# Down products of three feed-forward blocks: one 512-column matmul for both parts of the product, and its two halves added in two steps

## What is computed

```python
# first block
h = causal_dwconv(hn @ w_ffn_up[l], conv_w[l], conv_b[l])
x = x + (jax.nn.silu(h_gate) * h_val) @ w_ffn_down[l]
...
# second block, twice (g = g1 and g3)
x = x + 0.5 * g[:, None, :] * ((jax.nn.silu(gate) * up) @ w_out)
```

## Time and profile before

| | |
|---|---|
| median of 3 runs | 937.09 us (935.77 to 937.66) |
| profiled execution: time | 928.86 us |
| its span (first to last instruction) | 927.1 us |
| PE busy | 878.5 us (95%), 7320 matmul records |
| DVE busy | 710.3 us (77%) |
| ACT busy | 468.2 us (51%) |
| mean granted TensorE clock | 0.984 |
| w_lo (L1218) | x282, mean 1231 ns |
| w_hi (L841) | x282, mean 1052 ns |
| HBM read | 189.89 MB, 206 GB/s over the span |

### The profile page before, as it was taken

How to read it: one execution, slowest core, us unless ns; L and a number is a source line. 1 busy time by engine, 2 the same in 40 slices (tenths; PEclk the granted TensorE clock), 3 DMA queues, 4 the chain that set the end, 5 groups by cost and what they waited for, 6 DMA issues and landing times.

```text
span 927.1 us, 19318 instructions
## 1 busy us (share of the span) xinstructions
PE 878.5 (95%) x7320; PEld 842.5 (91%) x7320; DVE 710.3 (77%) x1104; ACT 468.2 (51%) x723; POOL 91.0 (10%) x139
## 2 busy tenths in 40 slices
PE   8999998999999988999999979899998979999996
PEld 6888997999999988999999869888998979999995
DVE  4898765999898778788888777678977878866543
ACT  5746654655664457334433455555643754434441
POOL 1022002000001320001012230000000200000010
PEclk9999999999999999899999999999999989999998
DMA  7453345566668974688889947745576347666651
GB/s 254 140 172 98 121 153 204 163 199 185 198 193 294 340 264 139 199 290 297 283 280 324 313 144 245 231 139 183 185 266 222 127 155 249 203 193 204 212 164 46
DMA packets 53334, 191.72 MB, mean 207 GB/s; under 512 B 5920, under 2 KB 6432, under 8 KB 53152
## 3 DMA queue, kind: packets, MB, share of 16 engines
q1 hardware_dynamic: 41760, 149.96, 49.1%
q0 software_dynamic: 10656, 39.33, 12.5%
q10 hardware_dynamic: 864, 1.67, 0.5%
HBM read 189.89 MB, written 1.05 MB: 206 GB/s over the span
## 4 chain that ended last, share of the span: by engine, by line
PE 76%; DVE 14%; ACT 5%; issue 3%; DMA 1%; SPq 0%; DVEq 0%; ACTq 0%
PE ps L388 22%; PE ps L390 22%; PE ps L389 22%; DVE w_lo L1218 5%; ACT w_hi L841 3%; DVE ada_raw L1520 2%; PE ps L460 1%; PE ps L462 1%; PE ps L461 1%; PE ps L496 1%; PE ps L553 1%; DVE rstd_w L1223 1%; DMA X<-x_in 1%; PE ps L527 1%; ACT xn L897 1%
## 5 line engine op out<-in xcount | busy, mean ns | idle before, releaser
L1218 DVE TENSOR_TENSOR w_lo<-raw,w_hi 128x1024 fp32r<-128x1024 f32 x282 | 342.0, 1231 | 114.2 <-ACT w_hi L841 113.8
L388 PE MATMUL ps<-xh,w_hi 128*128 128x256 f32 x1344 | 379.2, 282 | 19.2 <-DVE xl L1277 9.8
L389 PE MATMUL ps<-xl,w_hi 128*128 128x256 f32 x1344 | 374.8, 279 | 0.0
L390 PE MATMUL ps<-xh,w_lo 128*128 128x256 f32 x1344 | 374.7, 279 | 0.0
L841 ACT ACTIVATE w_hi<-raw 128x1024 fp32r<-128x1024 f32 x282 | 287.4, 1052 | 42.7 <-PE ps L390 38.8
L388 PEld LDWEIGHTS ps<-xh,w_hi 128*128 128x128 f32 x1344 | 255.8, 190 | 24.3 <-issue 21.1
L389 PEld LDWEIGHTS ps<-xl,w_hi 128*128 128x128 f32 x1344 | 255.5, 190 | 0.4 <-issue 0.2
L390 PEld LDWEIGHTS ps<-xh,w_lo 128*128 128x128 f32 x1344 | 255.2, 190 | 0.0
L388 PE MATMUL ps<-act_hi,w_hi 128*128 128x256 f32 x528 | 147.2, 279 | 5.0 <-DVE w_lo L1218 4.5
L390 PE MATMUL ps<-act_hi,w_lo 128*128 128x256 f32 x528 | 146.5, 277 | 0.0
L389 PE MATMUL ps<-act_lo,w_hi 128*128 128x256 f32 x528 | 146.5, 277 | 0.0
(11 more groups left out here) (259 smaller groups left out, 1140.8 us busy)
## 6 DMA issues: line engine op xcount, KB each, us to landing
raw<-w SPq DMA_DIRECT2D x282, 512.0 KB, 4.3
ada_raw<-ada_w POOLq DMA_DIRECT2D x72, 512.0 KB, 5.1
X<-x_in SPq DMA_DIRECT2D x4, 256.0 KB, 5.7
bm<-bias_in POOLq DMA_DIRECT2D x1, 1024.0 KB, 6.3
out<-X SPq DMA_DIRECT2D x4, 256.0 KB, 2.2
tab<-tab_in ACTq DMA_DIRECT2D x1, 640.0 KB, 4.2
gmask<-gmask_in ACTq DMA_DIRECT2D x1, 512.0 KB, 5.4
cact<-c_in POOLq DMA_DIRECT2D x1, 512.0 KB, 4.9
```

The lines of the kernel that those rows point to most:

```text
L388: pe.matmul(o, lh, rh, start=start, stop=False, skip_group_check=True)
L389: pe.matmul(o, lh, rl, start=False, stop=False, skip_group_check=True)
L390: return pe.matmul(o, ll, rh, start=False, stop=stop, skip_group_check=True)
L1218: v.tensor_tensor(w_lo[:, slot(h), :], raw[:, slot(h), :], w_hi[:, slot(h), :].bitcast(F32), ALU.subtract).then_inc(lo_ready, 1)
```

## The change

The two tensors act_hi and act_lo become one, `act`, in which the high and the low part of a hidden tile stand side by side (512 columns). PE multiplies w_hi by both with one matmul of 512 columns into the whole bank: columns 0 to 255 take w_hi x act_hi, columns 256 to 511 take w_hi x act_lo. The matmul w_lo x act_hi adds to columns 0 to 255 as before. So a weight tile has two matmuls and two weight loads in place of three, with 768 streamed columns as before, and the two halves of the bank have to be added together. That is done in `ffn_resid`: the left half is added to X, DVE waits for that addition to be complete, and then adds the right half to the same tile of X. Only the second addition signals `resid_done`, for which ACT's square waits.

```diff
-        ffn = phase([("act_hi", [P, FT, S], F32R), ("act_lo", [P, FT, S], F32R), ("cv", [P, 2, 2, SW], F32),
+        ffn = phase([("act", [P, FT, 2, S], F32R), ("cv", [P, 2, 2, SW], F32),
...
-        act_hi, act_lo, cv, sg, av, _, xr_h, xr_l, _, gain_sq, _, ada_raw, cact = ffn.values()
+        act, cv, sg, av, _, xr_h, xr_l, _, gain_sq, _, ada_raw, cact = ffn.values()
+        act_hi, act_lo = act[:, :, 0, :], act[:, :, 1, :]
...
-                    m = three(ffn_out(o), w_hi[:, slot(h), wc], w_lo[:, slot(h), wc], act_hi[:, ft, :], act_lo[:, ft, :], ft == 0, ft == FT - 1)
+                    pe.matmul(ps[:, 4 + o % 4, :], w_hi[:, slot(h), wc], act[:, ft, :, :].rearrange("p a n -> p (a n)"), start=ft == 0, stop=False, skip_group_check=True)
+                    m = pe.matmul(ffn_out(o), w_lo[:, slot(h), wc], act_hi[:, ft, :], start=False, stop=ft == FT - 1, skip_group_check=True)
...
-                if gate is None:
-                    v.tensor_tensor(X[:, o, :], ffn_out(o), X[:, o, :], ALU.add).then_inc(resid_done, 1)
-                else:
-                    v.scalar_tensor_tensor(out=X[:, o, :], in0=ffn_out(o), scalar=mod[:, gate, 16 + o:17 + o], in1=X[:, o, :],
-                                           op0=ALU.mult, op1=ALU.add).then_inc(resid_done, 1)
+                for part in range(2):
+                    src = ps[:, 4 + o % 4, part * S:part * S + S]
+                    if gate is None:
+                        ins = v.tensor_tensor(X[:, o, :], src, X[:, o, :], ALU.add)
+                    else:
+                        ins = v.scalar_tensor_tensor(out=X[:, o, :], in0=src, scalar=mod[:, gate, 16 + o:17 + o], in1=X[:, o, :],
+                                                     op0=ALU.mult, op1=ALU.add)
+                    if part == 0:
+                        own.mark(ins)
+                        own.wait()
+                ins.then_inc(resid_done, 1)
```

## The result

| | before | after |
|---|---|---|
| median of 20 runs each | 934.01 us (922.27 to 941.84) | 941.5 us (934.21 to 947.06) |
| ratio, with its 95% interval | | 1.012 (1.0096 to 1.0144) |
| profiled execution: time, span | 928.86, 927.1 us | 947.06, 945.3 us |
| mean granted TensorE clock | 0.984 | 0.981 |

The change makes the kernel slower by 1.2%, which on 934.01 us is 9.0 to 13.5 us; the two medians are 7.5 us apart, a ratio of 1.008, just outside that interval, so the size is less sure than the interval says. 943.9 us was forecast. The runs of one kernel spread by 1 to 2%, far more than the first three runs let me think. The profiled execution of the changed kernel is the slowest of its 20, and that of the kernel before is a quick one, so I read stages and not the 18.2 us between the two spans.

A forecast was written before the change was run, and what follows sets the result against it. A ring of DVE and ACT was taken to bound the first two down stages, PE the third. 3.2 + 3.8 + 0.5 - 0.7 = +6.8 us on a 937.09 us median gave 943.9 us, range 940.0 to 948.0.

The forecast's parts named there:

- the ring of ACT and DVE: First two down stages: addition, square, w_hi, w_lo set the pace, slower than PE; turns of 9.11 and 9.37 us.
- The second addition, first stage: First down stage: tiles 0 to 6 each pay 0.46 us ahead of PE's restart, tile 7 nothing; +3.2 us.
- Second stage: Second down stage: the second addition costs 0.52 us a tile, only 0.14 at tile 5 beside a transfer; +3.8 us.
- End of the third stage: Third down stage: only tile 7's second addition, behind PE's last matmul, costs; +0.5 us, tiles 0 to 6 hidden.
- The matmuls: Third down stage: a 512-column matmul takes 222 ns, a gain of 4 ns in each of 176 tiles; -0.7 us.
- The clock falls further: Rival: PE's longer waits bring more slow stretches, or wide matmuls cost 232 ns and later stages settle at 118; 947 us, chance 0.12.
- The layout: Writing act_hi and act_lo: same widths, same two instructions, only the distance between tiles changes; zero cost.
- In the first two stages the matmuls cost 0: First and second down stage: a faster PE only waits longer at the same w_lo; 0.
- PE decides after all: Rival: in the down stages additions lie beside PE except at stage ends, and matmuls gain; 931.6 us, chance 0.03.
- Half hidden: Rival: slots and transfers swallow most second-stage additions, or the first stage loses only its last tiles; 941 us, chance 0.12.
- It does not do what it says: Rival: the 512-column matmul runs as two of 256 at 226 ns, third stage gains nothing; 944.6 us, no separate chance.

The follow-up runs named there:

- e3: The kernel before with ACT's square of a finished tile moved behind the next w_hi, nothing else; 914.93 us, ratio 0.9842.
- e1: The changed kernel with three 256-column matmuls again, so only the second addition is left; 941.16 us against 929.43 for the kernel before, ratio 1.0127.
- e8: The changed kernel with a third DVE instruction that waits for the second addition and releases ACT in its place; 947.08 us in one run.
- run 20: Not a run label but a count: the kernel before, unchanged, was run 20 times; median 934.01 us.
- e2: The changed kernel with the 512-column matmul but only the first of the two additions; 932.45 us, ratio 1.0024 to the kernel before.
- e4: The changed kernel with ACT's square moved behind the w_hi of the next half; 925.4 us, ratio 0.9949 to the kernel before.
- e5: e4 with the wide matmul reading its 512 columns as two separate pieces; 927.29 us against 931.26 for the kernel before, ratio 0.9948.
- e9: e1 with ACT's square moved as in e3; 921.16 us against 930.93 for the kernel before, ratio 0.9886.
- e6: e4 with the w_lo matmul of each weight tile put in front of the wide one; 919.1 us in one run.
- e10: e3 again, the kernel before with the square moved, run beside e9; 916.98 us, ratio 0.9857 to the kernel before.
- e7: The kernel before profiled once more, without an edit; 931.31 us in one run.

## Why the prediction was right, and which term was mis-sized

**The bound.** That the ring of ACT and DVE sets the pace of the first two down stages, though PE holds 76% of the chain, is shown: take the square out of it and they are 3.1 and 5.3 us shorter (e3); lengthen it by 0.46 us and every turn grows by that (after, e1, e8).

**The second addition, first stage:** +3.2 forecast. PE's stage grew by 66.1 - 63.2 = 2.9 and the idle time behind it by 0.27, +3.2 together. Pair distance 0.46 and turn 9.56 (9.6 forecast) are as read from rows 3 and 8.

**Second stage:** +3.8 forecast. From the first scaling of X to the end of the last addition it was 539.3 - 484.0 = 55.3 us and is 555.3 - 495.6 = 59.7, +4.4. All eight additions are paid in full, 8 x 0.52 = 4.2: the 0.38 us of slack that I took off at tile 5 was not used. The turn is 9.88 (9.9 forecast). At the second transfer the wait stays, 1.15 us ahead of ACT's w_hi at 546.18 and 0.40 us on DVE behind it, as in rows 6 and 7:

```profile
546.18 1.06 ACT L843 ACTIVATE w_hi<-raw 128x1024 fp32r<-128x1024 f32 x1 [1.15 <-DMA raw<-w]
```

The transfer started later with the ring, as argued; it swallowed nothing of the additions ahead of it.

**End of the third stage:** +0.5 forecast, 1.00 - 0.48 = 0.52 in the row at 934.10. Additions of tiles 0 to 6 were to cost nothing there: e1's third stage is 59.5 us, as before.

**The matmuls: the step that failed in size, and in sign.** "I take 222 ns, a gain of 4 ns a tile: -0.7 us" was wrong. A wide and a narrow matmul take 353 ns, 13 more than three narrow ones at 113, and the third stage is 2.3 us longer. My upper bound, 232 ns, was the row at hand (rows 10), and I scaled it down because I held the slow speed for an effect of the stall in front. The error had two halves. The wide matmul is not at 232 but at about 235 ns, and the narrow one beside it does not stay at 113 but has 118, a case that I had put into the rival of the clock and not into the sum. With the terms as measured the sum is 3.2 + 4.4 + 0.5 + 2.3 = 10.4 us, inside 9.0 to 13.5; mine was 6.8, below it. That the median came out near the forecast owes something to chance: the kernel before, run 20 times, has a median 3.1 us below the 937.09 I started from, an error that works against the one in the sum.

The Trainium skill (TensorE: Matmul & The Clock Gate, Back-to-back issue gap) gives 215.8 ns for 512 columns at the full clock, by its formula for one matmul by itself. The trace does not agree: 61.8 us for 175 tiles leaves about 235 for the wide one. The prediction was right to stay above that, and not far enough.

**The layout** cost 0 as forecast: the two instructions that write it take 286 and 426 ns by their median, before and after.

**In the first two stages the matmuls cost 0,** as forecast, while the ring decides: e2 +0.1 and +0.5 us. That the wide matmul is slow comes out there only when the ring is gone (e4).

**The rivals.** *PE decides after all* falls with e1 and e3. *Half hidden* falls with the unchanged 1.84 and 1.44 us. *The clock falls further* was right in its second half (118 in the third stage) and wrong on the clock right behind the first stage (0.67 and 0.91). One more slow stretch did come, behind the second down stage (0.57 from 564 to 568 us). The three kernels with the longer ring (after, e1, e8) have one there in their profiles, the kernel before has none in either of its two; but e5 and e9, whose square is moved, have one as well, so the ring is not shown to be its cause. It had no price that can be seen: from the end of the second down stage to the first matmul of the third it is 316.4 us, and it was 317.1. *It does not do what it says:* the wide matmul runs as one record of 397 ns in place of two; that it takes 235 ns, twice the 117.5 of a slow narrow one, is what one would also see if the array went through it as two slow ones, and no run here tells these apart.

**What stays open:** why a stage with wide matmuls always has the slow speed. It is the width, or the mixture of widths; position (e5) and order (e6) are excluded, the granted clock is 1.00 throughout, and PE waits for nobody. What inside the chip sets one of the two speeds for a stage was not found. Open too is whether the longer ring has a part in the slow up stage behind it (after and e1, not e8): the 8.5 us that the additions cost in e1's stages lie just below the 8.6 to 15.0 us of its runs.

**The better version** is e3 (run again as e10): the kernel before with ACT's square behind the next w_hi, 0.984 and 0.986 of the time before. It beats both kernels.

## What to carry to other kernels

A busy PE can hide that it lives on a lead: look for idle time of the same length behind the same instruction on a helper engine, turn after turn, measure the turn against PE's work for it, and price a step in that ring by start-to-start distance. If work that nobody is waiting for (a square for a later norm) is queued in front of work that everybody waits for (the next weights), move it behind; here that one edit was worth more than the whole change cost. Before merging matmuls, measure the wide form in a full stream: here the same columns in fewer instructions took 353 ns a tile in place of 340.

## What the runs showed of the hardware that I had not expected

- The same stream of 256-column fp32r matmuls, with a weight load each, runs at 113 or at 117.5 ns, often a whole stage long, at a granted clock of 1.00 in both. Which one it gets changes from run to run (797 and 767 records in the same 90 us of the same code). An up stage of 100 us is 4 us longer in the slow case, which is as much as a whole term of the prediction, and a likely part of the spread of the runs. Where the speed changed inside a down stage, PE had just stood still. In e1's second down stage, ahead of a wait of 1.01 us and behind it:

```profile
L618 PE MATMUL ps<-act,w_hi x72: 281/281/281, 478.4 to 503.5; 128*128 128x256 f32 x72
L618 PE MATMUL ps<-act,w_hi x104: 276/276/286, 505.2 to 545.9; 128*128 128x256 f32 x104
```

In e7's second it went the other way, from 276 to 281 ns at a wait of 0.93 us ahead of 525.80. The chance seems to be drawn anew at such a stop; why it falls out as it does is not shown.
- 512-column fp32r matmuls with a 256-column one beside them took about 235 ns in each of 18 stages, twice the slow distance; the few in the kernel before that follow one another (rows 10) took 232.
- When the square moved, GpSimd's two products on it came to lie beside DVE's work, and both became slower. Before, they stand in DVE's idle time. GpSimd in e3 and, behind it, in the kernel before, one turn:

```profile
295.20 1.20 POOL L339 TENSOR_TENSOR xn<-xn 128x256 f32<-128x256 f32 x1
296.36 1.71 POOL L347 TENSOR_TENSOR gain_sq<-gain_sq 128x256 f32<-128x256 f32 x1
```

```profile
295.95 0.73 POOL L339 TENSOR_TENSOR xn<-xn 128x256 f32<-128x256 f32 x1
296.65 0.72 POOL L347 TENSOR_TENSOR gain_sq<-gain_sq 128x256 f32<-128x256 f32 x1
```

DVE's rows beside them have 1.77 and 1.75 us in place of 1.22 (the timeline of e3 above), 1.1 us a turn. In e3 that costs nothing that can be seen, since PE does not wait for w_lo; in e9, where DVE holds PE up, it may. The Trainium skill (SBUF — State Buffer, Who interferes with whom) says that a VectorE instruction with two inputs in SBUF contends with a GpSimd instruction that reads SBUF; the trace agrees, w_lo and the modulation's product being of that kind.
